# Two-block float32 transformer kernel: the first two weight strips after each matrix boundary are interleaved, and the norm's matmul follows both

## The chip, the cores and the metric

One NeuronCore of a Trainium2 chip runs the whole program. The metric is the device time of one execution in microseconds (us). Three runs of the kernel before took 1989.94, 1989.57 and 1992.37 us; the median is 1989.94 us.

## The reference, cut to what matters

Two model blocks run one after the other on a sequence of 512 tokens of width 1024, all in float32. The parts beside the change are these (the mixers between them are only named):

```python
# first block
h = h + mixed @ w_out
h = h + cross_attention(rms_norm(h, norm_x_g), rms_norm(mem, norm_mem_g), xa_wq, xa_wk, xa_wv, xa_wo)
h = h + square(relu(rms_norm(h, norm_ff_g) @ ff_w1)) @ ff_w2
x = rms_norm(h, final_norm_g)
# second block
h = rmsnorm(x, ln1_g)
proj = h @ w_in                      # 7 x 1024 columns, feeds a gated convolution and an RG-LRU
x = x + merged @ w_o                 # merged: two gated products with w_out_a and w_out_b
h = rmsnorm(x, ln2_g)
x = x + (silu(h @ w_ffn_gate) * (h @ w_ffn_up)) @ w_ffn_down
return rmsnorm(x, final_g)
```

## The kernel before

**Layout.** Activations stand transposed: features on the 128 partitions, the 512 tokens along the free dimension. A width of 1024 is eight tiles of 128x512, called contraction tiles 0 to 7. A weight matrix is cut into strips of 128 output columns; a strip holds eight 128x128 blocks, one for each contraction tile, 512 KB in all. There are 302 strips, in the order in which they are used.

**Split products.** float32 accuracy is had from rounded operands: every operand is split into a high and a low part, and TensorE runs three 128x128x512 matmuls for each contraction tile (L451 high by high, L452 high by low of the activation, L453 low of the weight by high). A strip is so 24 matmuls into one PSUM bank; four banks are used in turn, bank = strip mod 4.

**The ring of weights.** Four slots hold a strip each. For strip n, SyncE loads `raw` when TensorE has finished strip n-4 (`pe_done`); ScalarE copies it to `w_hi` (L855, in `high`); GpSimd subtracts to make `w_lo` (L419, in `low`) and raises `lo_ready`; TensorE starts strip n only when `lo_ready` is n+1. ScalarE's queue is in program order. Its helper `ahead(n)` makes the high part of strip n+3, and `root(n)` is the square root of a norm: it waits for VectorE's reciprocal. `squares(first, times)` is a loop of `ahead` over 4 strips.

**PSUM banks.** VectorE reads each finished strip out of its bank and counts in `evac`. Strip u of a matrix waits for `evac` to say that strip u-4 has been read (the argument `taken`).

**From one matrix to the next.** The output tiles of one matrix are the contraction tiles of the next. After WOUT, XO and WO2 `residual` (L1601 on) adds a strip's result to `h` (L1608), splits it into two tiles (L1151, L1153; the second raises `x_ready`), and squares and adds it for the norm (L1168, L1170). After the second product of the first feed-forward a longer loop (L1743 on) does the same and keeps a second sum of squares. The first strip of the next matrix waits tile by tile (`counts`), so it can begin on tiles 0 to 6 while tile 7 is still made. The RMS norm's scale is one number per token and is applied after the product: when all eight tiles have been squared, VectorE raises `norm_sum`, TensorE sums over partitions with a matmul against ones (`norm`, L479), VectorE scales the sum and takes the reciprocal (L1158, L1160; 3.35 us), ScalarE takes the root (L871), and only then can VectorE read the strips of the next matrix out of their banks.

**The boundaries.** There are six, and the letters are used below:

| boundary | from, to | norm? | what stands in ScalarE's queue there |
|---|---|---|---|
| A | WOUT to WQ | norm(2) | `w_hi` up to strip 2 of WQ, `root(2)`, then `w_hi` of strips 3, 4 ... |
| B | attention to XO | no | |
| C | XO to the first FF | norm(3) | `w_hi` up to strip 2 of FF, `root(3)`, an Exp for the LRU's constants, then `w_hi` of strips 3, 4 ... |
| D | FF to IN (the second block's input projection) | norm(4) and a second matmul, L807 | `w_hi` of strips 3 and 4 of IN, `root(4)`, `w_hi` of strip 5 ... |
| E | gated merge (MG) to WO2 | no | |
| F | WO2 to FFN | norm(5) | `w_hi` up to strip 2 of FFN, `root(6)`, then `w_hi` of strip 3, Silu ... |

At C VectorE computes about thirty tiny operations (L1679 to L1706) for the LRU's decay rate after the norm, and only then reads the first strip of FF (L1715). At D strip 2 of IN is no product with the normed input: it waits for `u_pair`, a tile that VectorE computes from strip 0's result, the norm's scale and four convolution taps (L1784, L1786, L1781, L1151, L1153). TensorE executes in program order, so it waits there too.

In the kernel before, TensorE's order at each boundary is: strip 0 (tile by tile as `x_ready` rises), the norm's matmul where there is one, strip 1, strip 2, strip 3 and so on. A helper `strip` issues one strip, `square` a whole matrix of eight.

Of the kernel before, what the change touches and what calls it, by code (L numbers as in the profile page):

```python
# [40 lines left out]
KT = D // P  # L41
MEM = 256
EPS = 1e-6
RING = 4
# [4 lines left out]
N_KV, N_SQ, N_FF, N_IN, N_MG, N_FFN = 16, 8, 64, 48, 32, 68  # L49
# [10 lines left out]
S_FF = S_XO + N_SQ  # L60
S_IN = S_FF + N_FF
# [15 lines left out]
E_FF = E_XO + N_SQ  # L77
E_IN = E_FF + N_FF
# [79 lines left out]
def build(nc, A, out):  # L158
    ctx = ExitStack()
    with ctx:  # L160
        def at(name, cols, offset, dt=F32):
            return nc.alloc_sbuf_tensor_at("m_" + name, [P, cols], dt, offset=SBUF0 + offset)

        def sem(name):
            return ctx.enter_context(nc.semaphore(name))
# [6 lines left out]
        XH = at("XH", KT * T, 64 * KB, F32R)  # L172
        XL = at("XL", KT * T, 80 * KB, F32R)
        YH = at("YH", KT * T, 160 * KB, F32R)
        YL = at("YL", KT * T, 176 * KB, F32R)
# [61 lines left out]
        e0 = at("e0", T, 192 * KB + 3584)  # L237
# [6 lines left out]
        ones = const[:, NCOL + P:NCOL + 2 * P]  # L244
# [13 lines left out]
        ps = ctx.enter_context(nc.psum_tensor("ps", [P, 8, T], F32))  # L258

        def tile(buf, k):  # L260
            return buf[:, k * T:(k + 1) * T]

        def tap(kind, half, k):

            n = (kind * 2 + half) * 2 * TT + k
            return tile(taps[0], n) if n < 28 else tile(taps[(n - 28) // 2 + 1], n % 2)
# [10 lines left out]
        lo_ready = sem("lo_ready")  # L277
        pe_done = sem("pe_done")
        evac = sem("evac")
# [21 lines left out]
        norm_two = sem("norm_two")  # L301
        norm_rstd = sem("norm_rstd")
        x_ready = sem("x_ready")
# [143 lines left out]
        def _(pe):  # L447
            def three(dst, slot, k, xh, xl, first, last):

                c = slice(slot * STRIP + k * P, slot * STRIP + (k + 1) * P)  # L450
                pe.matmul(dst, w_hi[:, c], xh, start=first, stop=False)  # L451
                pe.matmul(dst, w_hi[:, c], xl, start=False, stop=False)  # L452
                return pe.matmul(dst, w_lo[:, c], xh, start=False, stop=last)  # L453

            def strip(n, slot, bank, xh, xl, kt=KT, taken=None, needs=None, counts=None, width=T):

                pe.wait_ge(lo_ready, n + 1)
                if taken is not None:
                    pe.wait_ge(evac, taken)
                if needs is not None:  # L460
                    pe.wait_ge(*needs)
                for k in range(kt):
                    if counts is not None:
                        pe.wait_ge(counts[0], counts[1] + (k + 1))
                    mm = three(ps[:, bank, 0:width], slot, k, xh[:, k * width:(k + 1) * width],
                               xl[:, k * width:(k + 1) * width], k == 0, k == kt - 1)
                mm.then_inc(pe_done, 1)

            def square(s_first, e_first, xh, xl, ready=None, second=None):

                for u in range(N_SQ):
                    strip(s_first + u, (s_first + u) % RING, u % 4, xh, xl, taken=e_first + u - 3,
                          counts=ready if u == 0 else None)
                    if u == 0 and second is not None:
                        norm(second)

            def norm(n):
                pe.wait_ge(norm_sum, n)
                pe.matmul(ps[:, 7, :], ones, acc[:], start=True, stop=True).then_inc(norm_all, 1)  # L479
# [5 lines left out]
            for n in range(N_KV):  # L485
                if n < 8:
                    strip(n, n % RING, n % 4, NH, NL, taken=n - 3 if n > 3 else None,
                          counts=(mem_ready, 0) if n == 0 else None, width=MEM)
                elif n % 2:
# [6 lines left out]
                    for mt in range(2):  # L496
                        for k in range(KT):
# [4 lines left out]
                            mm = pe.matmul(dst, NL[:, a], both[0][:, :, k, :], start=False, stop=(k == KT - 1))  # L502
                    mm.then_inc(pe_done, 2)
                if n == 0:

                    pe.wait_ge(mem_sqr, 1)
                    for k in range(KT):
                        mm = pe.matmul(ps[:, 7, 0:MEM], ones, mem_sq[:, k * MEM:(k + 1) * MEM],
                                       start=(k == 0), stop=(k == KT - 1))
# [4 lines left out]
                if n == 3:  # L514
                    pe.wait_ge(norm_rstd, 1)
                    for mt in range(2):
                        mm = pe.matmul(ps[:, 6, mt:mt + 1], rstd[0:1, mt * P:(mt + 1) * P], ones[0:1, 0:1],
                                       start=True, stop=True)
                    mm.then_inc(mem_col, 1)
                if n in TAPS_AFTER:  # L520
# [7 lines left out]
                    for g in range(4):  # L528
                        mm = pe.matmul(ps[:, 4 + g, :], hid[0:64, tt * P:(tt + 1) * P],
                                       w3[0:64, g * T:(g + 1) * T], start=True, stop=True)  # L530
# [4 lines left out]
            for s in range(N_SPEC):  # L535
                n = S_SPEC + s
# [3 lines left out]
                for part in range(2 if s < 4 else 1):  # L540
                    for o in range(2):
                        for k in range(TT):
                            mm = three(ps[:, (s % 2) * 4 + part * 2 + o, :], n % RING, part * TT + k,
                                       tap(part, 0, o * TT + k), tap(part, 1, o * TT + k), k == 0, k == TT - 1)
# [53 lines left out]
            for q, src in enumerate((gA, gE)):  # L598
                if q:
                    pe.wait_ge(g_em, 1)  # L600
                for d in range(2):
                    for tt in range(TT):
                        c = q * 32 + (d * TT + tt) * 4
                        mm = pe.transpose(ps[:, 7, c:c + 4], src[0:4, d * T + tt * P:d * T + (tt + 1) * P],
                                          ident[0:4, 0:4])
# [57 lines left out]
            for o in range(2):  # L663
# [4 lines left out]
                for q, (kind, j) in enumerate(HY_ORDER):  # L668
                    n = S_HY + o * N_HY + (2 if kind == "I" else 0) + j // 2
# [5 lines left out]
                    if kind == "F":  # L675
                        if o or j >= 2:
                            pe.wait_ge(evac, E_HY + o * TT + j - 1)
                        for part in range(2):
                            half = (part + j // 2) % 2
                            for k in range(2):  # L680
                                mm = three(ps[:, b + part, :], n % RING, b * 2 + part * 2 + k,
                                           tile(ZH, k * 2 + half), tile(ZL, k * 2 + half), k == 0, k == 1)
                        mm.then_inc(pe_done if j % 2 else freq, 1)
                    else:
# [8 lines left out]
                        for part in range(2):  # L693
                            half = (part + j // 2) % 2
                            for k in range(2):
                                mm = three(ps[:, 4 + half * 2 + k, :], n % RING, b * 2 + part * 2 + k,
                                           tile(QH, 2 * j + part), tile(QL, 2 * j + part), j == 0, j == 3)
# [10 lines left out]
            for u in range(4):  # L708
                for k in range(4):
                    if u == 0:  # L710
                        pe.wait_ge(mixed, 4 + k + 1)
                    mm = three(ps[:, u, :], (S_WOUT + u) % RING, k, tile(XH, k), tile(XL, k), False, k == 3)
# [55 lines left out]
            attended(2)  # L768
            attended(3)
            square(S_XO, E_XO, XH, XL, (o_pair, 0))  # L770


            def ff_up(c, i):
                for u in range(4):
                    first = isinstance(c, int) and i == 0 and u == 0
                    strip(c * 16 + i * 4 + (S_FF + u), (S_FF + u) % RING, u, YH, YL,
                          taken=c * 16 + i * 4 + (E_FF + u - 3), counts=(x_ready, 2 * KT) if first else None)
                    if first:
                        norm(3)

            def ff_down(c):
                with pe.Fori(0, 2) as i:
# [10 lines left out]
                ff_down(c)  # L793


            def in_turn(i):

                for v in range(2):
                    for u in range(6):
                        w = v * 6 + u  # L800
                        if u != 2:
                            first = isinstance(i, int) and w == 0
                            strip(i * 12 + (S_IN + w), (S_IN + w) % RING, w % 4, XH, XL,
                                  taken=i * 12 + (E_IN + w - 3), counts=(x_ready, 3 * KT) if first else None)
                            if first:
                                norm(4)
                                pe.matmul(ps[:, 6, :], ones, e0[:], start=True, stop=True).then_inc(norm_two, 1)  # L807
                            continue
                        s = (S_IN + w) % RING
                        pe.wait_ge(lo_ready, i * 12 + (S_IN + w + 1))  # L810
                        pe.wait_ge(u_pair, i * 2 + (v + 1))
                        pe.wait_ge(evac, i * 12 + (E_IN + w - 3))
                        for g in range(2):
                            mm = three(ps[:, 4 + g, :], s, g, uH[:], uL[:], True, True)
                        mm.then_inc(pe_done, 1)
# [13 lines left out]
            s, e, done = S_FFN, E_FFN, 0  # L829
            for size in FFN_CHUNKS:  # L830
                if done == 0:
                    for u in range(4):
                        strip(s + u, (s + u) % RING, u, XH, XL, taken=e + u - 3,
                              counts=(x_ready, 4 * KT) if u == 0 else None)
                        if u == 0:
                            norm(5)
                with pe.Fori(0 if done else 1, size // 2) as i:
                    for u in range(4):
                        strip(i * 4 + (s + u), (s + u) % RING, u, XH, XL, taken=i * 4 + (e + u - 3))
                s, e = s + 2 * size, e + 2 * size  # L840
                with pe.Fori(0, 2) as i:
                    for u in range(4):
                        strip(i * 4 + (s + u), (s + u) % RING, u, FH, FL, kt=size, taken=i * 4 + (e + u - 3),
                              counts=(hidden, 32 + done) if u == 0 else None)
                s, e, done = s + 8, e + 8, done + size
# [1203 lines left out]
```

## Time and profile before

| | before |
|---|---|
| median of three runs | 1989.94 us (1989.57 to 1992.37) |
| span of the profiled execution, first to last instruction | 1990.6 us |
| instructions | 22223 |
| TensorE busy | 1780.5 us, 89% |
| VectorE busy | 1112.7 us, 56% |
| GpSimd busy | 758.5 us, 38% |
| ScalarE busy | 559.3 us, 28% |
| mean granted TensorE clock | 0.945 of full speed |
| data from HBM | 166.43 MB, 85 GB/s over the span |
| one strip: load, issue to landing (median) | 3.3 us |
| one strip: high part on ScalarE, low part on GpSimd (mean) | 1057 ns, 2467 ns |

The profile gives no other time for the profiled execution than its span, which lies 0.7 us above the median of the three runs. Busy time is the union of an engine's instructions. Matmuls are pipelined: one lasts 390 ns in the trace, but at full clock one starts every 227 ns. Where a row ends in square brackets, these hold the engine's idle time just before the instruction and what ended it.

### The profile page before, as it was taken

The numbers are of one execution on the slowest core, as the hardware profiler recorded it, in microseconds if no ns is written. First come the engines' busy times: TensorE is split into PE (matmuls) and PEld (weight loads), VectorE is DVE, ScalarE is ACT, GpSimd is POOL, SyncE is SP. The second block draws the span as 40 slices with busy tenths as digits, with TensorE's granted clock in tenths as the row PEclk, the third lists the DMA queues.
The fourth block names the chain that finished last, engine by engine and source line by source line (L and its number), as shares of the span: only waits on it lengthen the run. The fifth ranks groups of instructions, "written<-read, shape, count | busy, mean of one in ns | idle before, by whom it ended". The sixth has DMA issues, their size and how long they took to land.

```text
span 1990.6 us, 22223 instructions
## 1 busy us (share of the span) xinstructions
PE 1780.5 (89%) x7718; PEld 1438.9 (72%) x7718; DVE 1112.7 (56%) x1449; ACT 559.3 (28%) x670; POOL 758.5 (38%) x312
## 2 busy tenths in 40 slices
PE   6899989875889999999997788688999999999996
PEld 4677866654667677888885666566788888888885
DVE  5761487888773674415278667767633463233137
ACT  2322332232213121122111343333433233222221
POOL 3423431113332234444443334433444444444442
PEclk9899998987889999999997889889999999999998
DMA  4232220011321122222221222222222222232222
GB/s 152 85 116 75 96 73 34 33 43 42 117 74 54 63 75 90 100 95 95 95 95 63 76 83 85 84 74 87 93 95 95 95 95 95 99 101 96 95 95 95
DMA packets 47692, 169.27 MB, mean 85 GB/s; under 512 B 5204, under 2 KB 5204, under 8 KB 47320
## 3 DMA queue, kind: packets, MB, share of 16 engines
q1 hardware_dynamic: 44640, 160.45, 24.1%
q10 hardware_dynamic: 3000, 8.09, 1.2%
q8 instruction: 36, 0.59, 0.1%
q14 instruction: 16, 0.13, 0.0%
HBM read 166.43 MB, written 2.10 MB: 85 GB/s over the span
## 4 chain that ended last, share of the span: by engine, by line
issue 32%; PE 28%; POOL 14%; DVE 1%; POOLq 0%; ACT 0%; DVEq 0%
POOL m_w_lo L419 14%; PE ps L451 9%; PE ps L453 9%; PE ps L452 9%; DVE m_h L1906 0%; DVE m_s L1160 0%; POOLq L427 0%; POOLq L425 0%; POOL m_QL L439 0%; DVE m_qs L1532 0%; PE ps L479 0%; DVE m_qs L1534 0%; DVE m_ftmp L1524 0%; DVE m_ftmp L1522 0%; DVE m_s L1883 0%
## 5 line engine op out<-in xcount | busy, mean ns | idle before, releaser
L419 POOL TENSOR_TENSOR m_w_lo<-m_raw,m_w_hi 128x1024 fp32r<-128x1024 f32 x302 | 744.0, 2467 | 1156.8 <-ACT m_w_hi L855 1156.7
L855 ACT ACTIVATE m_w_hi<-m_raw 128x1024 fp32r<-128x1024 f32 x302 | 318.3, 1057 | 851.4 <-DMA m_raw<-in_strips 847.6
L451 PE MATMUL ps<-m_XH,m_w_hi 128*128 128x512 f32 x1160 | 471.7, 407 | 14.1 <-DVE m_XL L1153 11.8
L452 PE MATMUL ps<-m_XL,m_w_hi 128*128 128x512 f32 x1160 | 458.4, 395 | 0.0
L453 PE MATMUL ps<-m_XH,m_w_lo 128*128 128x512 f32 x1160 | 457.8, 395 | 0.0
L451 PEld LDWEIGHTS ps<-m_XH,m_w_hi 128*128 128x128 f32 x1160 | 223.2, 192 | 71.2 <-DVE m_XL L1153 13.6
L452 PEld LDWEIGHTS ps<-m_XL,m_w_hi 128*128 128x128 f32 x1160 | 222.7, 192 | 48.5 <-issue 2.7
L453 PEld LDWEIGHTS ps<-m_XH,m_w_lo 128*128 128x128 f32 x1160 | 221.9, 191 | 47.7
L451 PE MATMUL ps<-m_FH,m_w_hi 128*128 128x512 f32 x432 | 168.9, 391 | 3.0 <-DVE m_FL L1153 2.9
L452 PE MATMUL ps<-m_FL,m_w_hi 128*128 128x512 f32 x432 | 168.8, 391 | 0.0
L453 PE MATMUL ps<-m_FH,m_w_lo 128*128 128x512 f32 x432 | 168.6, 390 | 0.0
L451 PE MATMUL ps<-m_YH,m_w_hi 128*128 128x512 f32 x384 | 153.1, 399 | 11.0 <-DVE m_YL L1153 6.3
L452 PE MATMUL ps<-m_YL,m_w_hi 128*128 128x512 f32 x384 | 151.1, 393 | 0.0
L453 PE MATMUL ps<-m_YH,m_w_lo 128*128 128x512 f32 x384 | 150.9, 393 | 0.0
L451 PEld LDWEIGHTS ps<-m_FH,m_w_hi 128*128 128x128 f32 x432 | 81.5, 189 | 20.8 <-DVE m_FL L1153 3.8
L451 PEld LDWEIGHTS ps<-m_YH,m_w_hi 128*128 128x128 f32 x384 | 73.1, 190 | 28.9 <-DVE m_YL L1153 7.8
L453 PEld LDWEIGHTS ps<-m_FH,m_w_lo 128*128 128x128 f32 x432 | 81.5, 189 | 17.0
L452 PEld LDWEIGHTS ps<-m_FL,m_w_hi 128*128 128x128 f32 x432 | 81.4, 188 | 16.9
L452 PEld LDWEIGHTS ps<-m_YL,m_w_hi 128*128 128x128 f32 x384 | 73.2, 191 | 15.7 <-issue 0.8
L453 PEld LDWEIGHTS ps<-m_YH,m_w_lo 128*128 128x128 f32 x384 | 73.1, 190 | 15.5
L1730 DVE TENSOR_TENSOR m_h<-m_h,ps 128x512 f32 x24 | 16.5, 688 | 106.7 <-PE ps L453 106.7
L1880 DVE TENSOR_TENSOR m_s<-ps,m_rstd 128x512 f32<-128x512 f32 x22 | 15.2, 691 | 95.0 <-PE ps L453 95.0
(311 smaller groups left out, 2338.2 us busy)
## 6 DMA issues: line engine op xcount, KB each, us to landing
m_raw<-in_strips SPq DMA_DIRECT2D x302, 512.0 KB, 3.3
m_x_in<-in_x ACTq DMA_DIRECT2D x8, 256.0 KB, 4.0
m_x_res<-in_x ACTq DMA_DIRECT2D x1, 2048.0 KB, 7.9
out<-m_h SPq DMA_DIRECT2D x8, 256.0 KB, 2.1
m_memf<-in_mem ACTq DMA_DIRECT2D x1, 1024.0 KB, 10.1
m_decay<-in_decay ACTq DMA_DIRECT2D x1, 1024.0 KB, 15.2
m_w<-in_w ACTq DMA_DIRECT2D x1, 512.0 KB, 13.3
m_skip<-in_skip ACTq DMA_DIRECT2D x1, 512.0 KB, 3.8
```

The lines of the kernel that those rows point to most:

```text
L419: nc.gpsimd.tensor_tensor(w_lo[:, c], raw[:, c], f(w_hi[:, c]), ALU.subtract).then_inc(lo_ready, 1)
L451: pe.matmul(dst, w_hi[:, c], xh, start=first, stop=False)
L452: pe.matmul(dst, w_hi[:, c], xl, start=False, stop=False)
L453: return pe.matmul(dst, w_lo[:, c], xh, start=False, stop=last)
L855: act.activation(w_hi[:, c], raw[:, c], ACT.Copy).then_inc(hi_ready, 1)
L1730: dve.tensor_tensor(hm, hm, ps[:, u, :], ALU.add).then_inc(evac, 1)
L1880: dve.tensor_tensor(s0[:], ps[:, u, :], rstd[:], ALU.mult).then_inc(evac, 1)
```

## The change

A new helper `pair` takes the place of the first two calls of `strip` at each of the six boundaries. It issues contraction tiles 0 to 5 of strip 0, tiles 0 to 5 of strip 1, tiles 6 and 7 of strip 0 (which then raises `pe_done`), tiles 6 and 7 of strip 1 (`pe_done` again), and then the norm's matmul, which stood between strip 0 and strip 1. The two strips have a bank each, so both sums are open at once. The number of matmuls, their operands and all other engines' programs are unchanged.

```diff
+            def pair(n, banks, xh, xl, taken, ready, then=None):
+
+                for part, ks in enumerate((range(0, 6), range(6, KT))):
+                    for u in range(2):
+                        if part == 0:
+                            pe.wait_ge(lo_ready, n + u + 1)
+                            pe.wait_ge(evac, taken + u)
+                        for k in ks:
+                            if u == 0:
+                                pe.wait_ge(ready[0], ready[1] + k + 1)
+                            mm = three(ps[:, banks[u], :], (n + u) % RING, k, tile(xh, k), tile(xl, k),
+                                       k == 0, k == KT - 1)
+                        if part:
+                            mm.then_inc(pe_done, 1)
+                    if part and then is not None:
+                        then()
+
             def square(s_first, e_first, xh, xl, ready=None, second=None):
 
-                for u in range(N_SQ):
+                if ready is not None:
+                    pair(s_first, (0, 1), xh, xl, e_first - 3, ready, None if second is None else lambda: norm(second))
+                for u in range(0 if ready is None else 2, N_SQ):
                     strip(s_first + u, (s_first + u) % RING, u % 4, xh, xl, taken=e_first + u - 3,
                           counts=ready if u == 0 else None)
-                    if u == 0 and second is not None:
-                        norm(second)
...
             def ff_up(c, i):
-                for u in range(4):
-                    first = isinstance(c, int) and i == 0 and u == 0
+                first = isinstance(c, int) and i == 0
+                if first:
+                    pair(S_FF, (0, 1), YH, YL, E_FF - 3, (x_ready, 2 * KT), lambda: norm(3))
+                for u in range(2 if first else 0, 4):
...
+            def two_norms():
+                norm(4)
+                pe.matmul(ps[:, 6, :], ones, e0[:], start=True, stop=True).then_inc(norm_two, 1)
+
             def in_turn(i):
...
+                        if isinstance(i, int) and w < 2:
+                            if w == 0:
+                                pair(S_IN, (0, 1), XH, XL, E_IN - 3, (x_ready, 3 * KT), two_norms)
+                            continue
...
                 if done == 0:
-                    for u in range(4):
-                        strip(s + u, (s + u) % RING, u, XH, XL, taken=e + u - 3,
-                              counts=(x_ready, 4 * KT) if u == 0 else None)
-                        if u == 0:
-                            norm(5)
+                    pair(s, (0, 1), XH, XL, e - 3, (x_ready, 4 * KT), lambda: norm(5))
+                    for u in range(2, 4):
+                        strip(s + u, (s + u) % RING, u, XH, XL, taken=e + u - 3)
```

## Rows read from the trace of the kernel before

**Rows 1.** Waits of TensorE: total us, times, longest us.

```profile
PE ps L451 <- DVE m_uL L1153: 47.1, 6, 8.0
...
PE ps L451 <- DVE m_XL L1153: 11.8, 3, 6.2
...
PE ps L451 <- DVE m_YL L1153: 6.3, 3, 2.6
...
PE ps L451 <- DVE m_s L1715: 4.8, 1, 4.8
```

**Rows 2.** Timeline, boundary A: start us, us, engine, line, operation, operands, count.

```profile
571.32 0.50 PE L451 MATMUL ps<-m_YH,m_w_hi 128*128 128x512 f32 x1 [1.79 <-DVE m_YL L1153]
...
574.86 0.79 PE L451 MATMUL ps<-m_YH,m_w_hi 128*128 128x512 f32 x1 [2.57 <-DVE m_YL L1153]
...
578.39 0.80 PE L451 MATMUL ps<-m_YH,m_w_hi 128*128 128x512 f32 x1 [1.89 <-DVE m_YL L1153]
...
579.77 0.50 PEld L479 LDWEIGHTS ps<-m_acc,m_const 128*128 128x128 f32 x2 [0.45 <-DVEq L1616]
...
586.00 0.63 ACT L871 ACTIVATE m_rstd<-m_s 128x512 f32<-128x512 f32 x1 [20.68 <-DVE m_s L1160]
...
587.66 4.76 POOL L419 TENSOR_TENSOR m_w_lo<-m_raw,m_w_hi 128x1024 fp32r<-128x1024 f32 x2 [19.88 <-ACT m_w_hi L855]
```

**Rows 3.** Timeline of TensorE alone after boundary A: strip 1's and strip 2's last tiles.

```profile
587.27 0.39 PE L451 MATMUL ps<-m_YH,m_w_hi 128*128 128x512 f32 x1
...
592.71 0.39 PE L451 MATMUL ps<-m_YH,m_w_hi 128*128 128x512 f32 x1
```

**Rows 4.** Timeline, boundary C.

```profile
709.72 0.41 PEld L479 LDWEIGHTS ps<-m_acc,m_const 128*128 128x128 f32 x2
...
715.12 0.63 ACT L871 ACTIVATE m_rstd<-m_s 128x512 f32<-128x512 f32 x1 [10.02 <-DVE m_s L1160]
```

**Rows 5.** Timelines of GpSimd, VectorE and TensorE alone, boundary C.

```profile
718.30 7.10 POOL L419 TENSOR_TENSOR m_w_lo<-m_raw,m_w_hi 128x1024 fp32r<-128x1024 f32 x3 [12.03 <-ACT m_w_hi L855]
...
731.27 0.69 DVE L1715 SCALAR_TENSOR_TENSOR m_s<-ps,m_rstd 128x512 f32<-128x512 f32 x1 [0.47 <-DVE m_misc L1706]
...
732.11 0.77 PE L451 MATMUL ps<-m_YH,m_w_hi 128*128 128x512 f32 x1 [4.78 <-DVE m_s L1715]
```

**Rows 6.** Windows: PE busy (x) PEld busy (x) DVE busy (x) ACT busy (x) POOL busy (x), PEclk, DMA share, GB/s.

```profile
731.00:737.00 6.00, 4.89 (x12) 3.86 (x13) 5.30 (x5) 0.84 (x1) 2.36 (x1) 0.50 0.00 0
```

**Rows 7.** Timeline, boundary D.

```profile
1078.66 0.79 PE L451 MATMUL ps<-m_XH,m_w_hi 128*128 128x512 f32 x1 [6.17 <-DVE m_XL L1153]
...
1084.03 0.80 PE L451 MATMUL ps<-m_XH,m_w_hi 128*128 128x512 f32 x1 [3.73 <-DVE m_XL L1153]
...
1086.87 0.50 PEld L479 LDWEIGHTS ps<-m_acc,m_const 128*128 128x128 f32 x2 [1.91 <-DVEq L1752]
...
1094.88 0.63 ACT L871 ACTIVATE m_rstd<-m_s 128x512 f32<-128x512 f32 x1 [3.35 <-DVE m_s L1759]
...
1096.79 0.55 DVE L1786 TENSOR_SCALAR m_t<-m_pX,m_const 128x512 f32<-128x512 f32 x1 [0.30 <-DVE m_pX L1784]
...
1101.28 2.37 POOL L419 TENSOR_TENSOR m_w_lo<-m_raw,m_w_hi 128x1024 fp32r<-128x1024 f32 x1 [8.60 <-ACT m_w_hi L855]
...
1101.33 0.77 PE L451 MATMUL ps<-m_uH,m_w_hi 128*128 128x512 f32 x1 [4.55 <-issue]
```

**Rows 8.** One line, L1786: duration ns min/median/max, first and last start us.

```profile
L1786 DVE TENSOR_SCALAR m_t<-m_pX,m_const x8: 547/1998/2477, 1096.8 to 1364.0; 128x512 f32<-128x512 f32 x8
```

**Rows 9.** Timeline, boundary F.

```profile
1618.93 0.41 PEld L479 LDWEIGHTS ps<-m_acc,m_const 128*128 128x128 f32 x2
...
1624.33 0.63 ACT L871 ACTIVATE m_rstd<-m_s 128x512 f32<-128x512 f32 x1 [10.16 <-DVE m_s L1160]
...
1627.41 2.40 POOL L419 TENSOR_TENSOR m_w_lo<-m_raw,m_w_hi 128x1024 fp32r<-128x1024 f32 x1 [12.07 <-ACT m_w_hi L855]
```

**Rows 10.** Timeline of TensorE alone after boundary F: strip 2's last tile.

```profile
1630.26 0.39 PE L451 MATMUL ps<-m_XH,m_w_hi 128*128 128x512 f32 x1
```

More of the change, by code:

```diff
@@ L773, in ff_up @@
             def ff_up(c, i):
-                for u in range(4):
-                    first = isinstance(c, int) and i == 0 and u == 0
+                first = isinstance(c, int) and i == 0
+                if first:
+                    pair(S_FF, (0, 1), YH, YL, E_FF - 3, (x_ready, 2 * KT), lambda: norm(3))
+                for u in range(2 if first else 0, 4):
                     strip(c * 16 + i * 4 + (S_FF + u), (S_FF + u) % RING, u, YH, YL,
-                          taken=c * 16 + i * 4 + (E_FF + u - 3), counts=(x_ready, 2 * KT) if first else None)
-                    if first:
-                        norm(3)
+                          taken=c * 16 + i * 4 + (E_FF + u - 3))
             def ff_down(c):
@@ L800, in in_turn @@
                         w = v * 6 + u
+                        if isinstance(i, int) and w < 2:
+                            if w == 0:
+                                pair(S_IN, (0, 1), XH, XL, E_IN - 3, (x_ready, 3 * KT), two_norms)
+                            continue
                         if u != 2:
-                            first = isinstance(i, int) and w == 0
                             strip(i * 12 + (S_IN + w), (S_IN + w) % RING, w % 4, XH, XL,
[L804 to L807, printed above, removed]
+                                  taken=i * 12 + (E_IN + w - 3))
                             continue
```

## The prediction

> **What bounds the kernel now.** TensorE is busy 89% of the span and no other engine above 56% (the table above), so I first read the view of what TensorE waits for. It waits longest, 47.1 us, for `uL`, the LRU input of the IN stage. Among the lines that the change can reach are 11.8 us for `XL` (three times, most of it at boundary D), 6.3 us for `YL` (three times, all at A) and 4.8 us for L1715 (once, after C) [rows 1]. Then I read the timeline at each of the six boundaries, for three things: whether strip 0 waits for its tiles, when the norm's matmul is issued, and what is late after it.
>
> At **A** strip 0 waits before each of tiles 5, 6 and 7, for 1.79, 2.57 and 1.89 us: VectorE makes a tile every 3.5 us (574.86 - 571.32) and is behind [rows 2]. At **D** it waits 6.17 us before tile 6 and 3.73 before tile 7, since the loop there also keeps a second sum [rows 7]. At **B, C, E and F** the timelines show no wait for a tile: VectorE is done with tile 7 before TensorE asks for it. The interleaving can fill the waits at A and D alone; there is nothing to fill at the other four.
>
> The second thing to see is what hangs on the norm. At F the norm is issued at 1618.93, ScalarE's root starts 5.40 us later, at 1624.33, and the low part of strip 3's weights is written from 1627.41 to 1629.81 [rows 9]. GpSimd had stood idle for 12.07 us before it: the raw strip had landed, but ScalarE makes its high part behind `root` in program order, so **strip 3's weights follow the norm by 10.88 us** (1629.81 - 1618.93). TensorE needs them when strip 2 is done: its last tile starts at 1630.26 [rows 10], and a tile takes 5.44/8 = 0.68 us (5.44 us from 587.27 to 592.71 for a strip [rows 3]), so at 1630.94. That is 1.1 us of slack. At C the same delay is 718.30 + 2.37 - 709.72 = 10.95 us [rows 4, 5].
>
> **The change part by part.** It adds and removes no instruction on any engine but some semaphore waits of TensorE, whose cost I put at nothing: six boundaries, two waits each moved, and they are satisfied. What moves is strip 1's 24 matmuls, which now stand ahead of the norm, and strip 0's `pe_done`, which comes after 18 more matmuls (18 x 0.227 = 4.1 us). By the ring, that delays SyncE's load of strip 4. Strip 4 is not needed before strips 2 and 3 are done, 10.9 us after the pair, and a load, high part and low part take 3.3 + 1.06 + 2.47 = 6.8 us (the table above); I cost it at nothing. If that cover went, it would cost at most the 4.1 us once.
>
> *B and E: 0.* No norm, no tile waited for; the same 48 matmuls in another order. Bounds -0.3 and +0.3.
>
> *C: +5.4 us.* Strip 0 does not wait, so strip 1 is finished 5.44 us later than the norm was issued before, and the norm goes out at 715.16 instead of 709.72. Strips 0, 1, the norm and strip 2 end when they did. Behind the norm: root, Exp, strip 3's weights 10.95 us later, at 726.1, while TensorE is free for strip 3 at 709.72 + 1.1 + 2 x 5.44 = 721.7 (1.1 for the norm's two passes and their issue; an estimate from 709.72 and strip 4's wait, 732.11 - 4.78 = 727.3, which is three strips behind it and 1.3 us). So it newly waits 4.4 us. And strip 4 waits in any case for VectorE to read strip 0 out of its bank, which follows the norm through reciprocal, root and thirty tiny operations: L1715 ran at 731.27 and strip 4 started at 732.11 after 4.78 us of waiting [rows 5]. That whole chain starts 5.44 us later, so strip 4 starts at 737.5. The new wait of strip 3 lies inside this delay. What can alter it is how VectorE's tiny operations meet GpSimd's (one low part takes 2.4 us): bounds +4.4 (only strip 3's weights count) and +7.
>
> *F: +6.6 us.* The norm is issued 5.44 us later, at 1624.37; strip 3's weights are ready at 1629.81 + 5.44 = 1635.25; TensorE is free at 1630.94. It idles 4.3 us where it did not. Such a pause also costs clock: after 4.78 us of idling at C the granted clock was 0.50, i.e. 1.2 GHz, and in the window from 731 only 12 matmuls were started, with 4.89 us of busy time [rows 5, 6]. Full rate would have taken 11 x 0.227 = 2.5 us from the first start to the twelfth, the trace has some 4.8, so 2.3 us are lost. Sum 4.3 + 2.3 = 6.6; bounds 4.3 (no clock lost) and 7.5.
>
> *A: -1.2 us.* Strip 1's tiles 0 to 5 (4.1 us) fit behind tile 5 of strip 0: from 572.0 to 576.1. Tile 6 is then there, tile 7 at 578.39 as before, since VectorE does not depend on any of this [rows 2]. Three and six matmuls more, and the norm goes out at about 580.5 (with a full clock, 582.1 with half), against 579.77. Before, strip 1 came after it and its last tile started at 587.27, strip 2's at 592.71 [rows 3], so strip 3 started at 593.39. Now strip 3 could start near 587. But its weights hang on the root here too: root at 586.00 and low part ready at 587.66 + 2.38 = 590.04, i.e. 4.04 after the root [rows 2]. With the norm at 580.5 and 5.4 to the root, that is 589.9. Of the 5.44 us that strip 1 took behind the norm 3.5 arrive (593.4 - 589.9), and the pause of about 3 us before strip 3 costs clock again, which I take as at F: -3.5 + 2.3 = -1.2. Bounds -3.5 and +1.1 (norm at 582.1).
>
> *D: +3.0 us.* Here strip 1 was no cost: it ran while TensorE had to wait anyway, for strip 2's operand behind the norm; after strip 1 TensorE still idled 4.55 us, until 1101.33 [rows 7]. Filling the 6.17 us with it gains nothing, and only the time of the norm matters. It was issued at 1086.87. Now tile 7 of strip 0 and tiles 6 and 7 of strip 1, nine matmuls, stand between 1084.03 and the norm: after a pause of over 4 us at 0.43 us each, so until 1088.0, +1.1. Second, strip 1 finishes before the root and not after it, so strip 5's raw weights are there early and ScalarE makes their high part right behind the root. Its low part then runs from 1.66 to 4.04 us after the root's start (A's rows: 586.00, 587.66 [rows 2]). L1786 starts 1096.79 - 1094.88 = 1.91 after the root's start, in the middle. Before, that low part ran at 1101.28, clear of it [rows 7]. L1786 takes 547 ns alone and 1998 in the median, 2477 at most [rows 8]: I take it to be held until GpSimd is done, 4.04 - 1.91 = 2.1 plus some 0.3 instead of 0.55, i.e. +1.9. Sum +3.0; bounds -1.7 (norm not delayed and both norm matmuls at full clock, no meeting) and +3.5.
>
> **Sum:** -1.2 + 5.4 + 3.0 + 6.6 = **+13.8 us**. After each boundary TensorE is the bound again up to the next, so nothing takes the delay back. Against the profiled span 1990.6 + 13.8 = 2004.4; the median lies 0.7 below that span, so **2003.7 us**. The bounds added up are +3.5 and +19.1.
>
> **Rivals.**
>
> *The filled waits pay in full (faster).* The place is A: strip 1 is taken out of the path after the norm, 5.4 us, and C and F cost nothing. It decides at strip 3's weights: if they were ready no later than 5.44 + 1.1 us behind the norm, not 10.9, the later norm would be hidden by strip 2. Then 1989.9 - 5.4 = 1984.5 us. For it: strips up to 2 are ready at every boundary. Against it: GpSimd's 12.07 and 12.03 us of idling up to just behind the root [rows 5, 9]. The Trainium skill (Perfetto Trace Analysis, Optimization Strategies) asks to keep the matmul engine in use where it waits for others; by it alone this rival would be right; by the trace the idle time is there at A and D, but it is not what strip 3 waits for. Chance 0.05.
>
> *The boundaries cost less than I think.* The clock is not lost at A and F, tile 7 at D is met at full clock, and L1786 slips past: -3.5 + 4.4 - 1 + 4.3 = +4.2, 1994 us, up to 1997 with one of them. For it: 1.79 us of idling at A left the matmul after it at full rate. Against: 2.57 us did not. Chance 0.17, half of it near the limit of no change.
>
> *The delay spreads.* VectorE, later at C and D, meets GpSimd's low parts in FF and IN in worse places; eight turns of IN with up to 1.9 us each (L1786 again) would give 2010 to 2015. The eight turns show it meeting them in most cases already, so there is little left to lose. Chance 0.08.
>
> *My forecast*, 1998 to 2008: 0.70.
>
> **How the numbers follow.** A measurement of this kernel can tell some 0.2%, 4 us, from no change. Below 1986 lies only the first rival; within 4 us lie half of the second and a little of others: faster 0.05, same 0.10, slower 0.85. The range of 8 in 10 takes in my forecast with its bounds and most of the second rival: 1995 to 2009.
>
> **What would show it.** In the changed kernel's trace: no wait for a tile before strip 1's tiles at A and D; a new wait of L451 for `w_lo` L419, three times (A about 3 us, C 4.4, F 4.3); L1715 and strip 4 at C 5.4 us later behind the same strip 0; L1786 in its first turn over 2 us. The forecast is wrong if strip 3 at F starts with no wait for `w_lo`, or if the delay of the norm at C and F is less than 4 us.

## The result, and the profile after

The changed kernel took 2000.24 us in the median of 4 runs (1997.53 to 2002.97), the kernel before beside it on the same chip 1990.38 us. The ratio is 1.0047, with a 95% interval from 1.0031 to 1.0062: 6.2 to 12.3 us slower. The forecast was 2003.7, +13.8, which lies above that interval. One of the 23 executions of the kernel before that stand beside e1, e2, e3 and e5 took 2276 us at a granted clock of 0.742; it is in no ratio, since ratios compare undisturbed executions alone. The span of the changed kernel's profiled execution is 1995.7 us, only 5.1 us over that of before, so the traces are compared stage by stage and not by their spans.

The page's part 1, busy time by engine. Nothing was added:

```profile
span 1995.7 us, 22223 instructions
...
PE 1780.7 (89%) x7718; PEld 1439.5 (72%) x7718; DVE 1120.4 (56%) x1449; ACT 558.7 (28%) x670; POOL 756.8 (38%) x312
```

TensorE's waits in the changed kernel (total, times, longest), which answer to [rows 1]; the kernel's lines behind the new helper are 17 to 19 higher:

```profile
PE ps L451 <- DVE m_uL L1172: 46.4, 6, 7.9
PE ps L451 <- POOL m_w_lo L419: 22.4, 6, 7.8
...
PE ps L451 <- DVE m_XL L1172: 6.4, 2, 4.0
...
PE ps L451 <- DVE m_YL L1172: 3.1, 2, 1.8
...
PE ps L451 <- DVE m_s L1734: 2.9, 1, 2.9
```

The waits for tiles have shrunk as meant: `XL` from 11.8 to 6.4 us, `YL` from 6.3 to 3.1. In their place the waits for weights have grown from 11.9 us, three times, in the kernel before:

```profile
PE ps L451 <- POOL m_w_lo L419: 11.9, 3, 7.9
```

to 22.4 us, six times. TensorE's timeline at A, C and F shows the three new ones, 11.1 us together:

```profile
574.19 0.50 PE L451 MATMUL ps<-m_YH,m_w_hi 128*128 128x512 f32 x1 [1.33 <-DVE m_YL L1172]
...
576.37 1.02 PE L496 MATMUL ps<-m_acc,m_const 128*128 128x512 f32 x2
...
585.61 0.50 PE L451 MATMUL ps<-m_YH,m_w_hi 128*128 128x512 f32 x1 [2.74 <-POOL m_w_lo L419]
...
707.55 1.02 PE L496 MATMUL ps<-m_acc,m_const 128*128 128x512 f32 x2
...
718.29 0.80 PE L451 MATMUL ps<-m_YH,m_w_hi 128*128 128x512 f32 x1 [4.25 <-POOL m_w_lo L419]
...
729.70 0.47 PE L451 MATMUL ps<-m_YH,m_w_hi 128*128 128x512 f32 x1 [2.87 <-DVE m_s L1734]
...
1622.36 1.02 PE L496 MATMUL ps<-m_acc,m_const 128*128 128x512 f32 x2
...
1633.00 0.79 PE L451 MATMUL ps<-m_XH,m_w_hi 128*128 128x512 f32 x1 [4.14 <-POOL m_w_lo L419]
```

L496 is the norm's matmul (L479 before). Strip 3 waits 2.74, 4.25 and 4.14 us for its low part, 9.2, 10.7 and 10.6 us behind the norm. The timelines of ScalarE and GpSimd at F show the same order as [rows 9]: root, high part, low part.

```profile
1627.53 0.63 ACT L890 ACTIVATE m_rstd<-m_s 128x512 f32<-128x512 f32 x1 [15.71 <-DVE m_s L1179]
1628.18 1.28 ACT L874 ACT_TABLE_LOAD   x1
1629.47 1.06 ACT L874 ACTIVATE m_w_hi<-m_raw 128x1024 fp32r<-128x1024 f32 x1
...
1630.61 2.34 POOL L419 TENSOR_TENSOR m_w_lo<-m_raw,m_w_hi 128x1024 fp32r<-128x1024 f32 x1 [17.62 <-ACT m_w_hi L874]
```

At C L1734 (L1715 before) runs 21.3 us behind the norm's matmul, as it did before (731.27 - 709.95 there), and the norm is one strip later. Two windows from 1631, of the changed kernel and then of the kernel before, show what follows strip 3's pause at F, whose last 2.0 us lie in the first of them; the columns are those of [rows 6], the granted clock the third figure from the end:

```profile
1631.00:1637.00 6.00, 4.00 (x9) 3.14 (x10) 4.21 (x3) 3.35 (x4) 5.46 (x3) 0.60 0.11 44
```

```profile
1631.00:1637.00 6.00, 6.00 (x28) 4.99 (x27) 5.75 (x4) 0.54 (x2) 4.25 (x2) 1.00 0.27 87
```

The granted clock is 0.60 in the mean, i.e. mostly 1.2 GHz, against 1.00, and 9 matmuls are started instead of 28. In TensorE's timeline the first 14 matmuls behind the pause start some 0.43 us apart instead of 0.227, which is 2.9 us lost.

**Stage by stage.** Each kernel below is cut at the same events, taken from TensorE's timeline of its one profiled execution (us): the first matmul on tile 7 at A; the first matmul of XO; the first on tile 7 at D; the first on `uH` (strip 2 of IN); the matmul of the last norm.

| kernel | start to A | A, attention | C, FF | D | IN to last norm (F) |
|---|---|---|---|---|---|
| before | 578.39 | 82.16 | 423.48 | 17.30 | 875.34 |
| changed | 574.19 | 78.51 | 428.25 | 17.32 | 883.52 |
| order at A alone (e1) | 574.85 | 83.31 | 424.85 | 17.30 | 875.56 |
| order at C and F (e2) | 574.98 | 84.00 | 428.57 | 17.30 | 884.74 |
| norm behind strip 1 at C, F (e3) | 578.20 | 81.61 | 429.49 | 17.29 | 881.27 |
| norm behind strip 2 at C, F (e4) | 576.91 | 82.14 | 433.55 | 17.30 | 890.84 |
| changed, weights ahead of root (e5) | 580.91 | 76.84 | 424.40 | 18.01 | 876.10 |
| before, weights ahead of root (e6) | 579.07 | 81.84 | 419.79 | 17.29 | 875.16 |
| decay rate's operations moved (e7) | 578.10 | 84.40 | 415.69 | 17.29 | 875.47 |
| order at A, weights ahead, moved (e8) | 579.49 | 79.00 | 411.15 | 19.07 | 878.42 |
| order at D alone (e9) | 577.76 | 84.41 | 425.01 | 19.05 | 877.08 |
| weights ahead, moved, no new order (e10) | 575.37 | 81.94 | 411.25 | 17.19 | 876.32 |
| order at D, strip 5's weights later (e11) | 576.62 | 81.31 | 423.03 | 16.69 | 875.93 |

In the changed kernel's execution that makes -3.65 at A, +4.77 at C, 0.02 at D, +8.18 from IN on: +9.3 us in all from A on. The start to A was 4.2 us shorter, with no instruction changed there; over the 13 executions it lies between 574.2 and 580.9. That part is chance, and it explains why the spans differ by 5.1 only. Chance also moves the other stages: with nothing changed in it, C and FF took 423.0 to 425.0 us (before, e1, e9, e11), and the stretch from `uH` to the first strip of FFN 512.1 to 515.7 us (the kernels with the old order at E).

### The profile page after: what moved, and what is told of

Same layout as the page of the kernel before. It is cut to its first block, busy times and chain, and to the rows that moved or that the text cites. A ratio compares the mean times of both kernels' runs of the same rounds, so it can differ in the third digit from the quotient of the medians.

```text
span 1995.7 us, 22223 instructions
## 1 busy us (share of the span) xinstructions
PE 1780.7 (89%) x7718; PEld 1439.5 (72%) x7718; DVE 1120.4 (56%) x1449; ACT 558.7 (28%) x670; POOL 756.8 (38%) x312
## 4 chain that ended last, share of the span: by engine, by line
issue 40%; POOL 17%; PE 17%; DVE 1%; POOLq 0%; ACT 0%; DVEq 0%
POOL m_w_lo L419 17%; PE ps L451 6%; PE ps L452 6%; PE ps L453 6%; DVE m_h L1925 0%; POOLq L427 0%; POOLq L425 0%; DVE m_s L1179 0%; POOL m_QL L439 0%; DVE m_qs L1551 0%; DVE m_qs L1553 0%; DVE m_s L1902 0%; DVE m_ftmp L1543 0%; DVE m_ftmp L1541 0%; PE ps L496 0%
## 5 line engine op out<-in xcount | busy, mean ns | idle before, releaser
L453 PEld LDWEIGHTS ps<-m_YH,m_w_lo 128*128 128x128 f32 x384 | 73.2, 191 | 15.5
L451 PE MATMUL ps<-m_uH,m_w_hi 128*128 128x512 f32 x16 | 11.3, 707 | 66.7 <-DVE m_uL L1172 46.4
```

## The experiments

Each diff is against the kernel named. Times are medians of the runs, ratios those to the kernel before on the same chip with their 95% intervals.

**e1: the new order at A alone.** `pair` is called in `square` only where there is a norm; C to F are as before.

```diff
-                if ready is not None:
-                    pair(s_first, (0, 1), xh, xl, e_first - 3, ready, None if second is None else lambda: norm(second))
-                for u in range(0 if ready is None else 2, N_SQ):
+                if second is not None:
+                    pair(s_first, (0, 1), xh, xl, e_first - 3, ready, lambda: norm(second))
+                for u in range(0 if second is None else 2, N_SQ):
```

> The kernel before, with the new order at boundary A alone (WOUT to WQ; B to F as before). My theory (strip 3's weights hang on the norm's root, strip 1 leaves the path behind the norm): strip 3 of WQ starts 11.4 us after tile 7 was taken up instead of 15.0, as in the changed kernel, so 3.6 us less: ratio 0.998, and one new wait of about 2.7 us for the low part of the weights at strip 3. Rival (the filled waits pay in full): 5.4 us less, no new wait for weights. Rival (interleaving two sums costs by itself, or the later release of strip 0's slot is felt): no gain or a loss.

Measured 1990.97 us, 0.9984 (0.9972 to 0.9997): faster by 3.2 us, with 0.6 to 5.6 in the interval. In TensorE's timeline strip 3 starts 11.42 us after tile 7 was taken up, as forecast, against 15.0 before:

```profile
574.85 0.50 PE L451 MATMUL ps<-m_YH,m_w_hi 128*128 128x512 f32 x1 [1.30 <-DVE m_YL L1170]
...
586.27 0.51 PE L451 MATMUL ps<-m_YH,m_w_hi 128*128 128x512 f32 x1 [2.74 <-POOL m_w_lo L419]
```

The windows from 587 show what followed the pause of 2.74 us, first here and then in the changed kernel, where the pause was the same to the hundredth:

```profile
587.00:591.00 4.00, 4.00 (x13) 3.10 (x12) 0.00 (x0) 0.95 (x1) 4.00 (x3) 0.60 0.00 0
```

```profile
587.00:591.00 4.00, 4.00 (x20) 3.27 (x19) 0.00 (x0) 0.24 (x1) 4.00 (x3) 1.00 0.02 4
```

Here the clock went to 1.2 GHz for a while (0.60, 13 matmuls), there it did not (1.00, 20 matmuls). The scores (`K` by `Q`) are the first matmuls of attention. The scores' first matmul comes 40.36 us after tile 7 here and 38.77 there: 1.6 us hang on it, for the same code. In this one execution attention then took 3 us longer than before (42.95 us instead of 39.96 from the scores to XO; the unchanged attention of e2, e7, e8 and e9 took 41.6 to 41.7), so the row of the table shows no gain; the timed runs do, if barely.

**e2: the new order at C and F alone**, and **e3: no interleaving, only the norm's matmul behind strip 1 at C and F.** e2 has the lines of the change for `ff_up` and FFN; e3 against the kernel before is this:

```diff
-                    if first:
+                    if isinstance(c, int) and i == 0 and u == 1:
                         norm(3)
...
-                        if u == 0:
+                        if u == 1:
                             norm(5)
```

> The kernel before, with the new order at C and F alone. Theory (the norm goes out one strip later, 5.44 us, and everything behind it follows): +5.4 at C, +4.3 and some 2.3 us of lost clock at F, together +12, ratio 1.006. In the trace strip 3 of FF and strip 3 of FFN each wait 4.2 us for the low part of their weights, and strip 4 of FF starts about 5.4 us later behind the norm's old place. Rival (the loss lies in other places, at D or in a longer way of strip 4's load): under 4 us.

> No interleaving anywhere: at C and F strips 0 and 1 stay whole and in order, and only the norm's matmul is moved behind strip 1. Theory (it is the norm's place that costs): the same +12 us as with the interleaving at C and F, within 1.5 us, and the same two new waits of 4.2 us. Rival (the interleaving costs: strip 0's late pe_done, two open sums): near the time before, within 3 us.

Measured 2004.66 us, 1.0047 (1.0033 to 1.0061), and 2004.86 us, 1.0048 (1.0032 to 1.0064). The two are alike, and their waits in TensorE's timeline are the changed kernel's, here e3's:

```profile
725.40 0.79 PE L451 MATMUL ps<-m_YH,m_w_hi 128*128 128x512 f32 x1 [4.25 <-POOL m_w_lo L419]
...
736.83 0.77 PE L451 MATMUL ps<-m_YH,m_w_hi 128*128 128x512 f32 x1 [4.12 <-DVE m_s L1715]
...
1640.67 0.80 PE L451 MATMUL ps<-m_XH,m_w_hi 128*128 128x512 f32 x1 [4.14 <-POOL m_w_lo L419]
```

So the loss at C and F comes from the norm's place, and interleaving two sums costs nothing of its own that these runs could tell. The size was forecast at +12 and came out at 9.4 and 9.6 us by the ratio; 12 lies within both intervals.

**e4: the dose doubled.** As e3, with `u == 2` in both places: the norm goes out 10.9 us later than before.

> A double dose of the suspected cost: no interleaving, and at C and F the norm's matmul stands behind strip 2 instead of strip 0 (10.9 us later). Theory (everything behind the norm follows it one for one): at F strip 3 waits 4.2 + 5.44 = 9.6 us for its weights' low part, at C strip 4 starts 10.9 us later than in the kernel before; together about 5.4 + 5.4 us over the run with the norm behind strip 1, so 22 us over the kernel before, ratio 1.0112. Rival (the chain behind the norm has slack that one strip did not use up, or the loss is a fixed cost of a cold clock): less than 5 us more than with the norm behind strip 1.

Measured 2017.5 us, 1.0122 (1.0099 to 1.0144): +24.3 us, against +22 expected. Strip 3 waits at C and at F:

```profile
730.08 0.79 PE L451 MATMUL ps<-m_YH,m_w_hi 128*128 128x512 f32 x1 [9.73 <-POOL m_w_lo L419]
...
1652.36 0.80 PE L451 MATMUL ps<-m_XH,m_w_hi 128*128 128x512 f32 x1 [9.62 <-POOL m_w_lo L419]
```

9.73 - 4.25 and 9.62 - 4.14 are 5.48 both: one strip more is waited for one to one. In the table C and FF give +6.0 and +10.1 us for one and two strips, the part with F +5.9 and +15.5. Of the 15.5, 3.1 us lie ahead of F, between `uH` and the first strip of FFN (515.49 against 512.39 us), where nothing was changed; from there on it is 5.8 and 12.4 us.

**e5: the changed kernel with strip 3's high part ahead of the root**, and **e6: the same edit on the kernel before.** Both have this in ScalarE's program:

```diff
-            root(2)
-            squares(S_WQ, N_SQ // 4)
+            ahead(S_WQ)
+            root(2)
+            for u in range(1, N_SQ):
+                ahead(S_WQ + u)
...
+            ahead(S_FF)
             root(3)
...
+            ahead(S_FFN)
             root(6)
```

(the loops behind them begin one strip later).

> The changed kernel, and in ScalarE's queue the high part of strip 3 stands ahead of the norm's root at A, C and F instead of behind it. Theory (program order on ScalarE is what makes strip 3 late): no wait for the low part at strip 3 of WQ, FF and FFN; A gains 2.7 us more, F loses nothing any more (6.6 us back), C keeps its +5.4 us, which come through VectorE's constants and the bank of strip 0. Together 9 us under the changed kernel: about 0.5 us around the kernel before. Rival (strip 3's weights are late because their load or GpSimd is late): the waits stay and the time is that of the changed kernel, +10 us.

> The kernel before, with the high part of strip 3 ahead of the norm's root in ScalarE's queue at A, C and F. Theory (in the kernel before strip 1 and 2 covered the chain of norm, root and strip 3's weights, with 1.1 us to spare at F): no change, within 2 us. Rival (the order of ScalarE's queue is worth something by itself): over 3 us faster.

e5 took 1992.12 us, 0.9995 (0.9982 to 1.0008): in the sum the changed kernel's loss is gone. No strip 3 waits for weights at A, C or F any more. From the norm of F to the last one it is 352.24 us against 359.43 in the changed kernel; before, with the norm one strip (5.44 us) earlier, 357.51, so F now costs 352.24 + 5.44 - 357.51 = 0.2 us. At A the stage is 5.3 us shorter than before, but 1.7 of that lie in the unchanged attention (38.28 us from the scores to XO instead of 39.96). From tile 7 to the scores it is 38.55 us, against 42.20 before and 38.77 in the changed kernel: the wait of 2.74 us has gone, and in its place the matmuls behind tile 7 ran slow (nine starts, 2.0 us lost, against 0.3 in the changed kernel). Strip 4 at C follows the norm as ever, 22.2 us behind it (712.57 to 734.79), and since strip 3 no longer fills that time all of it is seen as a wait:

```profile
734.79 0.76 PE L451 MATMUL ps<-m_YH,m_w_hi 128*128 128x512 f32 x1 [10.28 <-DVE m_s L1750]
```

Yet C and FF took 424.40 and not 428: from strip 4 on it was 3.7 us less than in the changed kernel (329.21 against 332.91 us to the first strip of IN), 2.9 of it a wait for a hidden tile (`FL`, the low part of what stands between FF's two products), which both kernels without the edit have and e5 has not. Why that wait went is open. So e5 removes the cause at F, and what makes up for C in its sum is A's gain and this wait. e6 took 1992.83 us, 0.9993 (0.9979 to 1.0007): no change that can be told from zero, as forecast. Its trace shows a gain that I had not looked for, though. Strip 4 at C waits only 0.52 us:

```profile
728.22 0.47 PE L451 MATMUL ps<-m_YH,m_w_hi 128*128 128x512 f32 x1 [0.52 <-DVE m_s L1731]
```

VectorE's tiny operations met GpSimd's low parts twice there, in VectorE's timeline:

```profile
718.75 2.35 DVE L1709 TENSOR_SCALAR m_misc<-m_misc 128x8 f32<-128x8 f32 x1
...
721.74 2.25 DVE L1709 TENSOR_SCALAR m_misc<-m_misc 128x8 f32<-128x8 f32 x1
```

Alone they take 0.17 us. In e5, as in the kernel before and the changed one, there are four such meetings, and two more of them are the difference between 22.16 us from the norm to strip 4 before and 17.90 in e6. How often they meet is not settled by the order alone.

**e7: the decay rate's tiny operations moved** from behind the norm at C to the place before the last quarter of FF (`hidden_chunk(3)`).

```diff
-            dve.wait_ge(sp_exp, 1)
-            ch.add(dve.tensor_scalar(m[2], m[1], 2.0, None, ALU.add))
...
             with ch.loop(3, 16) as c:
...
+            dve.wait_ge(sp_exp, 1)
+            ch.add(dve.tensor_scalar(m[2], m[1], 2.0, None, ALU.add))
...
             hidden_chunk(3)
```

> The kernel before, with VectorE's tiny operations for the LRU's decay rate moved from behind the norm at C to the place before the last quarter of FF. Theory (at C the bank of strip 0, and so strip 4, waits for them, and the wait costs clock): strip 4 of FF no longer waits 4.8 us, and 2.3 us of slow matmuls go: 7 us faster, ratio 0.9965. Rival (at their new place they are in the way of VectorE's work on the last quarter of FF, or meet GpSimd more often): less than 3 us, with a new wait in FF.

Measured 1985.76 us, 0.9948 (0.9929 to 0.9966): 10.4 us faster, 7.8 of it in the stage of C and FF. No wait of strip 4 is left. The forecast was 7 us, which lies within the interval (6.8 to 14.2).

**e8: everything that helps**, and **e10: the same without the new order.** e8 is e1, the order of e6 and the move of e7; e10 is e6 and e7.

> All that the theory says should help, on the kernel before: the new order of matmuls at A alone, the high part of strip 3 ahead of the root at A, C and F, and the decay rate's operations moved. Theory: 5.4 us at A (3.6 and the 2.7 us wait for weights, less what the clock gives back), 7 us at C, nothing at F: 12.5 us under the kernel before, ratio 0.9937. If only the 3.6 us at A and 7 at C arrive: 10.6 us, 0.9947.

> The same as the run with all three, but with no interleaving at all: the kernel before with the high part of strip 3 ahead of the root and the decay rate's operations moved. Theory (the interleaving at A is worth 5.4 us once strip 3's weights are there): 7 us under the kernel before, and 5.4 us over the run with the interleaving at A. Rival (the interleaving gives nothing that the order of ScalarE's queue does not give): the two are within 1 us.

e8 took **1977.35 us, 0.9915 (0.9894 to 0.9935)**: 17 us under the kernel before, and 26 under the changed one by the two ratios (23 by the medians). e10 took 1981.15 us, 0.9942 (0.9920 to 0.9965), 11.6 us under the kernel before. Both gained more than forecast: 12.5 us were expected of e8, just outside its interval of 13.0 to 21.1, and 7 of e10. Between the two lie 0.0027, 5.4 us, the size expected for the interleaving at A, but their intervals overlap, so the runs alone do not prove it. From tile 7 at A to the scores e8 needs 37.34 us, e10 41.99: 4.6 us less, where the nine executions without the new order at A lie between 41.46 and 42.75. The two also gain 4.5 us more in C and FF than e7 alone; TensorE's waits for hidden tiles sum up to 3.2 us in e7, to 0.3 in e10 and to 0.1 in e8. The wait that has gone is one of 2.9 us in FF; the slow matmuls around it, 1.6 us, went too. I had not expected that, and why the wait goes in e5, e8 and e10 but not in e6 and e7 is open.

**e9: the new order at D alone**, and **e11: e9 with the high part of strip 5 behind the two sigmoids** instead of behind the root.

```diff
-                            ahead(S_IN + i * 12 + v * 6 + u)
+                            if (v, u) != (0, 2):
+                                ahead(S_IN + i * 12 + v * 6 + u)
...
                             act.activation(t2[7][:], t2[7][:], ACT.Sigmoid).then_inc(lru_s, 1)
+                            if isinstance(i, int) and v == 0:
+                                ahead(S_IN + 2)
```

> The kernel before, with the new order at D alone. By the changed kernel's trace (17.32 us from tile 7's first matmul to strip 2, against 17.30 before): two effects that cancel. Behind the waits that strip 1 fills, the norm's two matmuls run at full clock and VectorE gets its sums 1.9 us earlier; and L1786 meets GpSimd's low part of strip 5 and takes 2.4 us instead of 0.55. So no change of the time, within 2 us, and 17.3 us in the trace. My recorded step said +3.0: then 20.3 us.

> As the run with the new order at D alone, but ScalarE makes strip 5's high part behind the two sigmoids and not right behind the root, so that GpSimd's low part comes later than L1786. If the two effects are what I say: L1786 takes 0.55 us in its first turn, and from tile 7's first matmul to strip 2 it is 15.5 us instead of 17.3. Rival (VectorE was slow for another reason, or the gain was not the clock's): 17.3 as before.

e9 took 1992.86 us, 1.0001 (0.9989 to 1.0014), e11 1994.74, 1.0005 (0.9992 to 1.0017): no change in time, either of them. The traces tell more. L1786 (L1805 in the changed kernel, L1807 in e9, L1810 in e11) in its first turn, in VectorE's timelines of the three:

```profile
1091.90 2.37 DVE L1805 TENSOR_SCALAR m_t<-m_pX,m_const 128x512 f32<-128x512 f32 x1 [0.30 <-DVE m_pX L1803]
```

```profile
1099.87 2.37 DVE L1807 TENSOR_SCALAR m_t<-m_pX,m_const 128x512 f32<-128x512 f32 x1 [0.30 <-DVE m_pX L1805]
```

```profile
1093.11 0.55 DVE L1810 TENSOR_SCALAR m_t<-m_pX,m_const 128x512 f32<-128x512 f32 x1 [0.30 <-DVE m_pX L1808]
```

With GpSimd out of the way it takes 0.55 us, and D is 16.69 instead of 19.05 us. L1786's 1.8 us are most of that; another 0.5 is the norm's matmuls, which passed quicker in e11. The two miss my 15.5 and 17.3 by 1.2 and 1.8 us, both for one reason in the main: tile 7 met a slow clock, and the norm came 1.17 us later. In the changed kernel it met a full one. These two rows are tile 7's matmul there and in e11:

```profile
1080.95 0.50 PE L451 MATMUL ps<-m_XH,m_w_hi 128*128 128x512 f32 x1 [2.37 <-DVE m_XL L1172]
```

```profile
1080.96 0.79 PE L451 MATMUL ps<-m_XH,m_w_hi 128*128 128x512 f32 x1 [4.40 <-DVE m_XL L1177]
```

The norm's matmul followed 2.84 us later there (1083.79), 4.01 us later in e11.

## Why the prediction was right, and where its sizes were off

The sign, the mechanism and the place were as forecast; +13.8 us was forecast and 6.2 to 12.3 measured, so the sum was too large. In the trace it is 9.3, and the 4.5 us between come from A (2.4) and D (3.0), less 0.9 from C, F and the rest.

**B and E: 0.** No run isolates them, but the trace does: the first four strips take 22.21 us at B, 22.20 before, and 21.76 at E in both, with no wait. The rest in the last stage (8.18 less F's 7.4) is 0.8 us, and lies within what chance does there.

**C: +5.4.** L1734 and strip 4 follow the norm by the same time as before (22.15 us from norm to strip 4, 22.16 before), and the norm is one strip later. The stage gave +4.8, +5.1 in e2 and +6.0 in e3, around 5.4 by less than the 2 us by which it varies unchanged. The two doses fit the one-to-one rule. That it was VectorE's constants that set strip 4 was shown by e7.

**F: +6.6.** From the norm to the last one 359.43 us, to 357.51 before, plus the strip: 7.4 us in the changed kernel, 6.1 in e2, 5.8 in e3. The wait was 4.14 (forecast 4.3), the rest clock: behind this pause, the same to the hundredth, the slow starts cost 2.9 us in the changed kernel, 1.7 in e2 and 1.5 in e3 (forecast 2.3). e5 removed the cause, ScalarE's program order, and with it F's loss.

**A: -1.2.** This is the first term that was mis-sized: the strip 3 that was ready 3.5 us earlier held (15.0 to 11.42 us), but the 2.3 us of clock behind its pause did not come. It measured -3.65 in the stage, -3.4 of it up to the scores, and -3.2 in e1's runs, where the clock took 1.6 us in the profiled execution and left -1.8 up to the scores; e1's interval holds the forecast too. I had taken the clock's price from a pause of 4.78 us and used it for one of 3.

**D: +3.0.** The second: 0.0 in the changed kernel, +1.75 in e9's trace, and no change in e9's time. L1786 was held as forecast, 2.37 us instead of 0.55. But the nine matmuls before the norm ran at full clock in the changed kernel, behind a pause of 2.37 us before tile 7 and not of over 4: the filled time had lasted longer than I had reckoned. The reading of D had left out a wait before tile 5 (1.88 us in the kernel before). In the changed kernel's execution it was longer. These rows are VectorE's, GpSimd's and TensorE's there:

```profile
1067.31 2.86 DVE L1172 SCALAR_TENSOR_TENSOR m_XL<-m_h,m_misc,m_XH  x1
...
1067.28 2.34 POOL L419 TENSOR_TENSOR m_w_lo<-m_raw,m_w_hi 128x1024 fp32r<-128x1024 f32 x1 [3.08 <-ACT m_w_hi L874]
...
1070.22 0.80 PE L451 MATMUL ps<-m_XH,m_w_hi 128*128 128x512 f32 x1 [4.05 <-DVE m_XL L1172]
```

VectorE's operation for tile 5 ran beside GpSimd's subtraction (2.86 us instead of 0.75), TensorE paused 4.05 us before tile 5, and the matmuls behind that pause ran slow: 10.73 us from tile 5 to tile 7 (1070.22 to 1080.95) held 8.36 us of work. In e9 and e11, with pauses of 1.91 and 1.74 us before tile 5, the same stretch of 12.93 us held 7.63 and 6.02 us of work and two pauses, the second of them 4.40 us. So the norm was not late at all, and its matmuls were quicker: from the norm to the root it took 6.21 us instead of 8.01. That quicker passage, which the forecast carried only in its lower bound, came in e9 (6.77) and e11 (6.24) too, where the norm was 1.17 us late as forecast. In the changed kernel it pays for L1786: from the root to strip 2 it took 8.27 us instead of 6.45.

**The rivals.** That filled waits pay in full was wrong by the 2.7 us that strip 3 waited at A and by all of C and F. Its point of decision was right, however: with the weights there in time, A gave 4.6 us up to the scores (e8 against e10), of the 5.4 that it named. The Trainium skill (Perfetto Trace Analysis, Optimization Strategies) sets the goal of keeping the matmul engine in use; A in e8 agrees, while C and F show that the order that serves it at one boundary costs time at another. The rival of smaller costs was near for D and A. The spreading delay was not seen in the IN turns: L1786's seven later turns took 13.5 us in all, 14.1 before.

## What to carry to other kernels

When work is moved ahead of an instruction that other engines wait for, ask what hangs on that instruction and by how much its cover shrinks: here two strips of cover stood over a chain of 10.9 us, and one was taken away at four norms, two of which had no gap to fill. Interleave only where the timeline shows TensorE waiting for tiles, and look in each in-order queue for work that is ready and stands behind a wait: putting one strip's `w_hi` ahead of the root took 7.2 us back at F, and with A's gain and a wait in FF that went the sum was that of the kernel before. Small operations on a critical chain can cost more than their own time; thirty of 0.17 us held up strip 4 by 4.8 us, since four of them took over 2.2 us each beside GpSimd.

## What the runs showed of the hardware that I had not expected

- The clock after a pause is not a matter of the pause alone. The same 2.74 us at A was followed by full clock in the changed kernel and by 0.60 in e1; 4.40 and 2.37 us before tile 7 at D gave half and full. The same 4.14 us at F cost 2.9, 1.7 and 1.5 us of slow starts in three executions. Such terms should be carried as a range, here from 0 to 2.9 us. What decides within it, these runs do not show.
- A VectorE operation that reads and writes only SBUF can last as long as a GpSimd subtraction that runs beside it: 0.17 us operations took 2.35, L1786 took 0.55 or 2.37 by where strip 5's low part lay. In e8 it was the operation that makes `uL`, 2.88 us instead of 0.69, and D took 19.07 us. Operations that read PSUM, such as the first read of a strip, kept their time: of 394 on tiles of 128x512 in the kernel before none took over 0.81 us, while of 666 with all operands in SBUF (reciprocals and scans left out) 157 took over 1 us. The Trainium skill (SBUF — State Buffer, Who interferes with whom) says that the two engines share a pair of ports as an exclusive lock; these rows agree.
- Unchanged code varied by more than expected from one execution to the next: 574.2 to 580.9 us to A, 38.3 to 43.0 from the scores to XO.
